# Row products of U on three places of their own, three picks moved to the later part of the pass, a buffer of its own for the last block

## The reference

```python
q = (xb @ w_q).reshape(T, PEER_HEADS, 2, PEER_QDIM // 2)
s = jnp.einsum('thpc,hpkc->thpk', q, sub_keys)          # scores against 2 x 128 keys per head
top_s, top_i = lax.top_k(s, PEER_TOPK)                  # 16 best keys of each half
cand = top_s[:, :, 0, :, None] + top_s[:, :, 1, None, :]
best_s, best_c = lax.top_k(cand.reshape(T, PEER_HEADS, PEER_TOPK * PEER_TOPK), PEER_TOPK)
ids = i1 * N_KEYS + i2                                  # 8 heads x 16 experts for each token
g = jax.nn.softmax(best_s, axis=-1)
act = jax.nn.gelu(jnp.einsum('td,thkd->thk', xb, u_tab[ids]), approximate=False)
out = jnp.einsum('thk,thkd->td', g * act, v_tab[ids])
```

## Time and profile before

| | us |
|---|---|
| median of 3 runs | 2987.31 (2981.48 to 2988.35) |
| the profiled execution, its own time | 2983.09 |
| its span, first to last instruction | 2981.3 |
| TensorE busy | 2801.1 (94%) |
| VectorE busy | 2345.2 (79%) |
| GpSimd busy | 1576.7 (53%) |
| ScalarE busy | 969.3 (33%) |
| mean granted TensorE clock | 0.964 of full speed |

### The profile page before, as it was taken

One profiled execution on the slowest core, in us unless ns is written; L12 is line 12 of the kernel. 1 busy time (PEld: TensorE's weight loads), 2 busy tenths in 40 slices (PEclk: granted clock), 3 DMA queues, 4 the chain that ended last, 5 costly groups with the idle time before them and its releaser, 6 DMA issues.

```text
span 2981.3 us, 33747 instructions
## 1 busy us (share of the span) xinstructions
PE 2801.1 (94%) x12016; PEld 2151.1 (72%) x12016; DVE 2345.2 (79%) x3821; ACT 969.3 (33%) x1331; POOL 1576.7 (53%) x1235
## 2 busy tenths in 40 slices
PE   7999689999688899999979999999999999999998
PEld 3546544788567688888767777777777777777776
DVE  2787943587999977777568888888888888888886
ACT  2014232311144466666222323223223223232233
POOL 1999400011011265666157777777777777777640
PEclk9999589999899999999989999999999999999999
DMA  3111010212335599999998888889888888898883
GB/s 121 39 46 54 3 43 0 78 43 78 130 121 170 162 332 366 366 362 362 351 339 304 301 305 317 296 301 317 301 303 310 300 306 308 298 320 288 317 290 142
DMA packets 253976, 685.16 MB, mean 230 GB/s; under 512 B 31984, under 2 KB 97648, under 8 KB 248432
## 3 DMA queue, kind: packets, MB, share of 16 engines
q0 software_dynamic: 104448, 335.81, 32.4%
q1 hardware_dynamic: 83568, 313.65, 28.6%
q10 hardware_dynamic: 65792, 33.56, 3.9%
HBM read 611.60 MB, written 71.30 MB: 229 GB/s over the span
## 4 chain that ended last, share of the span: by engine, by line
PE 66%; DVE 24%; DVEq 3%; issue 2%; DMA 2%; ACT 2%; another core or an unknown queue 1%; SPq 0%; ACTq 0%
PE ps L1604 21%; PE ps L1596 14%; PE ps L1569 11%; PE ps L1527 6%; DVE ps L1214 6%; DVE hnT L895 4%; PE ps L1455 3%; PE ps L1555 3%; PE ps L1364 2%; DVE ul L1187 2%; DVE wl L1284 1%; PE ps L1324 1%; DMA u_raw<-in_uT 1%; DVE lx L1061 1%; PE ps L1419 1%
## 5 line engine op out<-in xcount | busy, mean ns | idle before, releaser
L523 POOL DMA_INDIRECT vring<-in_v_tab,idsA x512 | 547.3, 1069 | 323.9 <-DVE ps L1214 193.9
L1214 DVE SCALAR_TENSOR_TENSOR ps<-vring,hsel,ps 128x1024 f32<-128x1024 f32 x508 | 652.0, 1283 | 15.3 <-DVE ps L1214 0.5
L512 POOL DMA_INDIRECT hsel<-hidden,idsE x384 | 436.8, 1138 | 159.8 <-issue 109.0
L1604 PE MATMUL ps<-vh,wh 128*128 128x512 f32 x1024 | 403.8, 394 | 28.4 <-DVE wl L1284 28.4
L1596 PE MATMUL ps<-xh,uh 128*128 128x512 f32 x1024 | 408.3, 399 | 12.0 <-DVE ul L1187 11.4
L1604 PE MATMUL ps<-vh,wl 128*128 128x512 f32 x1024 | 405.7, 396 | 0.0
L1596 PE MATMUL ps<-xh,ul 128*128 128x512 f32 x1024 | 405.1, 396 | 0.0
L1604 PE MATMUL ps<-vl,wh 128*128 128x512 f32 x1024 | 403.6, 394 | 0.0
L1596 PE MATMUL ps<-xl,uh 128*128 128x512 f32 x1024 | 402.7, 393 | 0.0
L1569 PE MATMUL ps<-hx,xh 128*128 128x512 f32 x768 | 314.5, 410 | 52.9 <-DVE lx L1061 51.6
L498 POOL TENSOR_TENSOR hot<-marks,selG 128x1024 f32<-128x1024 bf16 x64 | 140.1, 2190 | 364.6 <-PE ps L1555 227.0
(11 more groups left out here) (187 smaller groups left out, 4960.7 us busy)
## 6 DMA issues: line engine op xcount, KB each, us to landing
xraw<-in_uX SPq DMA_DIRECT2D x128, 512.0 KB, 6.5
u_raw<-in_uT SPq DMA_DIRECT2D x128, 512.0 KB, 7.3
v_raw<-in_v_tab SPq DMA_DIRECT2D x128, 512.0 KB, 5.4
gates<-gbuf ACTq DMA_DIRECT2D x16, 2048.0 KB, 23.7
gt<-gates SPq DMA_DIRECT2D x32, 1024.0 KB, 7.6
hidden<-hst SPq DMA_DIRECT2D x96, 256.0 KB, 8.1
wqbuf<-in_w_q SPq DMA_DIRECT2D x16, 512.0 KB, 3.4
vring<-in_v_tab,idsA POOLq DMA_INDIRECT x512, 5.8
```

The costliest lines, as they stand in the source:

```text
L512: nc.gpsimd.indirect_dma_start(out=hsel[:, n, k:k + 1], out_offset=None, in_=hidden_items, in_offset=bass.IndirectOffsetOnAxis(ap=idsE[:, ...
L523: nc.gpsimd.indirect_dma_start(out=vring[r % VS][:, :], out_offset=None, in_=v_rows if r >= P else u_rows, in_offset=bass.IndirectOffsetOn ...
L1214: nc.vector.scalar_tensor_tensor(out=bank2(6), in0=vring[slot][:, :], scalar=w, in1=bank2(6), op0=ALU.mult, op1=ALU.add).then_inc(cb_done, 1)
L1604: last = mm(ps[:, 2 + k % 4, :], w[:, c, tt * P:(tt + 1) * P], v[:, c, dh * 512:(dh + 1) * 512], start=c == 0 and w is wh and v is vh, sto ...
```

## The change

1. **Picks.** `picks_done` now spreads five picks (tiles 0, 4, 5, 6, 7; 70 steps) over quarters 0 to 35, and the other three (tiles 1, 2, 3; 42 steps) over quarters 36 to 121.
2. **Hot blocks** stand five quarters later: 21 + 1.5 n, quarters 21 to 115.
3. **Dots** run from quarter 41 to 126, 1.49 a quarter. Their rows have three places (`uring`, the places 2, 4 and 6 of `vring`) instead of eight, and semaphores of their own (`u_got`, `dot_read`). The fetch of a dot stands two quarters before it in GpSimd's list, and from the fourth on it waits until the dot three before it is done. The fetches of V rows count from zero again and begin when all dots are done.
4. **Last block.** The results of block 31 of the pass go to a buffer of their own, `hlast`, and the store has a semaphore of its own. So the first piece of the gates (`gt`, which lies where `hst` was) is loaded before these stores and no longer behind them.
5. `exps` stands one quarter earlier in ScalarE's list relative to its pick; some small tiles (`cand2`, `idf`, `best`, ...) have other addresses. The way back of `xh` and `xl` stays behind the stores of block 29 in SP's list.

```diff
-PICK_QUARTERS = 44
-X_BLOCK = PICK_QUARTERS // QB - 1
-X_QUARTER = PICK_QUARTERS + 4
+FIRST_PICKS = 1 + HT
+FIRST_QUARTERS = 36
+LAST_PICK = QUARTERS - 6
+X_BLOCK = FIRST_QUARTERS // QB - 1
+X_QUARTER = FIRST_QUARTERS + 4
 DOT_FROM = X_QUARTER + 1
+DOT_SLOTS = (2, 4, 6)
+US = len(DOT_SLOTS)
...
-def picks_done(qb):
-    return min(NT * STEPS_PICK, NT * STEPS_PICK * (qb + 1) // PICK_QUARTERS)
+def picks_done(Q):
+    first = FIRST_PICKS * STEPS_PICK
+    if Q < FIRST_QUARTERS:
+        return first * (Q + 1) // FIRST_QUARTERS
+    return min(NT * STEPS_PICK, first + (NT * STEPS_PICK - first) * (Q + 1 - FIRST_QUARTERS) // (LAST_PICK - FIRST_QUARTERS))
...
 def hot_quarter(n):
-    return 16 + n * 3 // 2
+    return 21 + n * 3 // 2
...
+        uring = [vring[k] for k in DOT_SLOTS]
+        hlast = at(0, "hlast", [P, PT, WIDTH])
...
             def store_hidden(B):
                 for n in range(PT):
                     e = B * PT + n
                     sp.wait_ge(h1_free, e + 1)
-                    sp.dma_start(hidden[n * P:(n + 1) * P, B * WIDTH:(B + 1) * WIDTH],
-                                 hst[:, e % HSLOTS, :]).then_inc(hst_out[e % HSLOTS], 16)
+                    dst = hidden[n * P:(n + 1) * P, B * WIDTH:(B + 1) * WIDTH]
+                    if B == NB - 1:
+                        sp.dma_start(dst, hlast[:, n, :]).then_inc(hlast_out, 16)
+                    else:
+                        sp.dma_start(dst, hst[:, e % HSLOTS, :]).then_inc(hst_out[e % HSLOTS], 16)
...
                 if B == NB - 1:
                     for c in range(2):
                         sp.wait_ge(lx_ready, QUARTERS - QB + c + 1)
                         sp.dma_start(u_raw[:, c, :], uT[c]).then_inc(u_in[c], 16)
+                    for slot in range(HSLOTS):
+                        sp.wait_ge(hst_out[slot], 16 * stores(slot))
+                    load_gates(0)
                 store_hidden(B)
-                if B == hot_quarter(HT * BLOCKS - 1) // QB + 2:
+                if B == hot_quarter(HT * BLOCKS - 1) // QB + 1:
...
-            def gather_row(r):
-                if r >= VS:
-                    pool.wait_ge(cb_done, r - VS + 1)
-                elif r == VS - 2:
+            def gather_dot(k):
+                if k == 0:
+                    pool.wait_ge(ids_ready, 1)
+                    pool.wait_ge(sel_ready, FIRST_PICKS)
+                elif k >= US:
+                    pool.wait_ge(dot_read, k - US + 1)
+                else:
                     pool.wait_ge(xt_ready, 1)
...
                 nc.gpsimd.indirect_dma_start(
+                    out=uring[k % US][:, :], out_offset=None, in_=u_rows,
+                    in_offset=bass.IndirectOffsetOnAxis(ap=idsA[:, 0, k:k + 1], axis=0)).then_inc(u_got[k % US], 16)
...
-                while Q > X_QUARTER - 3 and rows < min(ITEMS, items_done(Q + 3)):
-                    gather_row(rows)
-                    rows += 1
+                for k in range(P):
+                    if quarter_of_dot(k) - 2 == Q:
+                        gather_dot(k)
...
             def dot(k):
-                dve.wait_ge(v_got[k % VS], 16 * (k // VS + 1))
-                row = vring[k % VS][:, :]
+                dve.wait_ge(u_got[k % US], 16 * (k // US + 1))
+                row = uring[k % US][:, :]
                 nc.vector.scalar_tensor_tensor(out=row, in0=row, scalar=1.0, in1=bank2(6), op0=ALU.mult, op1=ALU.mult,
-                                               accum_out=hsel[:, 0, k:k + 1]).then_inc(cb_done, 1)
+                                               accum_out=hsel[:, 0, k:k + 1]).then_inc(dot_read, 1)
```

More of the change, by code:

```diff
@@ L110, with stores @@
 AX = mybir.AxisListType
-def picks_done(qb):
-    return min(NT * STEPS_PICK, NT * STEPS_PICK * (qb + 1) // PICK_QUARTERS)
+def picks_done(Q):
[3 more added lines that the diff above has]
+    return min(NT * STEPS_PICK, first + (NT * STEPS_PICK - first) * (Q + 1 - FIRST_QUARTERS) // (LAST_PICK - FIRST_QUARTERS))
 def quarter_of_step(k):
-    return next(qb for qb in range(PICK_QUARTERS) if picks_done(qb) > k)
+    return next(Q for Q in range(QUARTERS) if picks_done(Q) > k)
+def stores(slot):
+    return len(range(slot, (NB - 1) * PT, HSLOTS))
 def share(total, parts, n):
@@ L126, in hot_quarter, with dots_done, quarter_of_dot @@
 def hot_quarter(n):
-    return 16 + n * 3 // 2
-def items_done(Q):
-    return min(ITEMS, share(ITEMS, QUARTERS - 1 - DOT_FROM, max(0, Q + 1 - DOT_FROM)))
-def quarter_of_item(r):
-    return next(Q for Q in range(QUARTERS) if items_done(Q) > r)
+    return 21 + n * 3 // 2
+def dots_done(Q):
+    return min(P, share(P, QUARTERS - 1 - DOT_FROM, max(0, Q + 1 - DOT_FROM)))
+def quarter_of_dot(k):
+    return next(Q for Q in range(QUARTERS) if dots_done(Q) > k)
 def row_of_step(step):
@@ L375, in load_x, with load_gates @@
                 sp.dma_start(xraw[:, r, :, :], uX[b, :, r * KQ:(r + 1) * KQ, :]).then_inc(xraw_in[r], 16)
+            def load_gates(g):
+                sp.dma_start(gt[:, :, :, :], gates[g]).then_inc(g_in, 16)
             def store_hidden(B):
@@ L440, in load_group @@
                     sp.dma_start(v_raw[:, c % VR, :], v_tab[g * GC + c]).then_inc(v_in[c], 16)
-                    if c == (0 if first else 1):
-                        if first:
-                            for slot in range(HSLOTS):
-                                sp.wait_ge(hst_out[slot], 16 * (NB * PT // HSLOTS))
-                        else:
-                            sp.wait_ge(w_ready, g * GC)
+                    if c == 1 and not first:
+                        sp.wait_ge(w_ready, g * GC)
                         load_gates(g)
@@ L1254, in _ @@
                     marked += 1
-                for r in range(items_done(Q - 1) if Q else 0, items_done(Q)):
-                    if r < P:
-                        dot(r)
-                    else:
-                        combine(r - P)
+                for k in range(dots_done(Q - 1) if Q else 0, dots_done(Q)):
+                    dot(k)
             for c in range(2):
```

74 lines of the change are left out of this document (39 added, 35 removed).

## The result

| | before | after |
|---|---|---|
| median, us | 2984.39 (2980.73 to 2988.35, 4 runs) | 2945.44 (2939.84 to 2955.07, 4 runs) |
| ratio, 95% interval | | 0.9874 [0.9848, 0.9901] |
| the profiled execution, its own time | 2983.09 | 2955.07 |
| its span | 2981.3 | 2953.3 |

The change gains 39 us, 1.3%, and the interval keeps clear of no change; 2950 us was forecast. The profiled execution is the slowest of its four runs and gains 28 us. So I use a second profiled execution of the same program as well, taken beside the experiments ("after again", own time 2945.49). Of these two the second stands for the median.

A forecast was written before the change was run, and what follows sets the result against it. VectorE's picks were taken to bound quarters 4 to 43 and TensorE quarters 43 to 126. The terms, 42 − 8 + 0 + 3 = 37 us, put the median at 2950 us, range 2933 to 2975.

The forecast's parts named there:

- term 2: Three places for U rows, quarters 41 to 126: the loop of three dots loses 8 us, bounds 0 to 35.
- Term 1: Picks moved out of quarters 4 to 43: quarter 43 starts at 994, 42 us gained, bounds 36 to 47.
- are hidden: Later quarters: VectorE's idle 1.3 us a quarter covers the 42 moved steps, 0.9 us a quarter (75 us).
- mean P = 10.9: Mean time of one turn of three dots, in us; turns were to cost nothing up to 10.7.
- Term 3: Load of quarter 127 behind the last gates piece: piece takes 32 us, wait stays 5 us, change 0, bounds +6 and −21.
- my formula: Before quarter 127: TensorE waits if the last gates piece takes over 26.9 us to land.
- Term 4: Hand-over to the next pass: `gt` no longer waits behind the last stores, 3 us gained, bounds 0 and 5.
- The ring, mildly: Rival: fetches land after 9.8 to 10 us, the three places lose 26 to 35 us, 2968 to 2977; chance 0.12.
- Badly: Rival: a turn of three dots takes over 11.8 us, slower than before, 3007 us at 12.2; chance 0.08.
- Late gates: Rival: the last gates piece takes 53 us again, TensorE waits 26 us before quarter 127, 2971 us; chance 0.09.
- VectorE bounds the later part: Rival: scalings and picks collide or uneven steps keep TensorE waiting, 20 us of the picks' gain lost, 2970; chance 0.07.

The follow-up runs named there:

- repeats, 8 places: Changed kernel without picks of tiles 1 to 3, with 64 repeated `lx` operations in quarters 41 to 120 and eight places: 3052.7 us, ratio 0.9869.
- dots by time: Changed kernel with 116 dots in quarters 41 to 115 and 12 in quarters 116 to 126: 2944.19 us, ratio 0.9879.
- gates behind stores: Changed kernel with the first load of `gt` back behind the last three stores and the wait for them: 3060.14 us, ratio 0.9899.
- repeats, 3 places: Changed kernel without picks of tiles 1 to 3, with 64 repeated `lx` operations in quarters 41 to 120, three places: 3061.77 us, ratio 0.9898.

## Why the prediction was right, and where it was wrong

The total was right, but partly by luck: term 2 was mis-sized (−21 us for −8), and terms 1, 3 and 4 together came out better than forecast by about as much. With −21 in term 2 and the other terms as forecast the gain would have been 24 us. In the second execution (span 37.6 us shorter) the terms measure as follows; the profiled first one in brackets.

**Term 1, the picks that move: 42 forecast, +49.0 (+46.3) measured.** Quarter 43 starts at 987.3 (990.0) instead of 994, with 15 blocks done as said: 54.3 us earlier less three blocks of 1.78. In the first execution the first wait for `lx` was 16.35 us, 17 forecast, and all of TensorE's waits up to 1041.6 us together 19.9, under 30:

```profile
787.43 0.80 PE L1592 MATMUL ps<-hx,xh 128*128 128x512 f32 x1 [16.35 <-DVE lx L1087]
```

Only two short ones follow it. Quarter 36 started at 948.9 (951.7) us, 956 forecast, so my 1.78 us a step and 3 us for uneven steps together were a little too dark; the second execution is 2 us above the upper bound of 47.

**The moved steps "are hidden": this and term 2 is where the working failed.** The idle 79.6 us of the earlier trace rows were counted twice: once as cover for 42 steps, once as VectorE's freedom to start up to three quarters ahead while the ring turns. The ring without the late picks is free up to quarter 116 (0.2 us of excess); with them, or with plain operations of the same length, the excess is some 10 us above before. Work without the narrow ring was not free either in the one run that has it (repeats, 8 places: 6.8), so how the 10 us split between the two is not shown. A late row holds VectorE up, and what stands behind it, now with a pick step among it, no longer catches up before TensorE asks.

**Term 2, the three places: −8 forecast, −21.0 (−28.5) measured,** within its bounds (0 to −35). I put into it all that TensorE lost between quarter 43 and 127, though the late picks have a part in it. It is the excess up to quarter 116, 9.8 (11.4) above before, and that of quarters 116 to 127 without a wait at 127, 11.2 (17.0) above before. Fetches landed after 8.2 us, in the 7 to 9 forecast, and GpSimd did wait for dots. What I had wrong is the part of the ring in the tail. There TensorE needs only 8.3 us for three dots; I named that number and yet laid the whole of it into one mean P = 10.9 over 43 turns. The median hid that fetches in the chain of the tail landed after 6.6 to 15.9 us (first execution); the 15.87 one was issued 1.1 us behind the first of the two 2 MB loads:

```profile
1427.50 0.74 SPq L439 DMA_DIRECT2D xh<-x_rows  x1
1428.29 0.81 SPq L440 DMA_DIRECT2D xl<-x_rows  x1
```

My own test for this was "quarter 126 ends more than 15 us behind quarter 43's start + 437": it ended 22.6 (30) behind. By that test I was wrong.

**Term 3, the way to quarter 127: 0 forecast, +5.7 (+4.9) measured,** near its upper bound of +6. The last piece of the gates was issued at 1396.23 and landed after 27.9 us, 32 forecast and 53.3 before:

```profile
gates<-gbuf ACTq DMA_DIRECT2D x1, 2048.0 KB, 27.9
```

The limit for no wait was 26.9 us, so by my formula 1 us was to be left, and 0.87 was. That match is luck. The load of quarter 127 was issued at 1429.5 and took 20.2 us, so it had landed by 1449.7; the 0.87 us are the end of the wait for a late row, whose dot at 1455.33 stands in VectorE's list before the `lx` at 1456.69. TensorE came 11 to 17 us later to quarter 127 than its own work needs, so the load had that much more time. Where TensorE does not lose that time, the wait before quarter 127 is there: 8.54 and 6.45 us without late picks (3 and 8 places), 7.99 in "dots by time", 8.75 in "repeats, 8 places", against 5.73 before. So terms 2 and 3 don't add up independently: the ring's loss in the tail hides a wait for this load of 6 to 9 us. What the change cost the tail is better read as one number: excess 11.4 (18.1) against 5.9.

The Trainium skill (DMA: Bandwidth & Descriptors, "Queues, rings and completion order") has each DMA engine take turns between queues with work; by that rule three places were to bring this term to +6. The piece did land sooner, but runs made for other questions show that it needs no three places. With the new tables, eight places and no late picks the last piece landed after 31.7 us, though the 15 row fetches from 1369 to 1393 us took 8.8 to 17.0. And with three places and the old tables it was issued at 1418.3, and its queue moved nothing more from 1450 on, so under 32 us. Either change alone goes with some 32 us instead of 53.3; why, these runs don't separate further.

**Term 4, the hand-over: +3 forecast, about +4.3 measured:** 2.1 us from quarter 127 to the first matmul with U, 2.2 us from there to the first with V. Only the second half is what I had forecast, and "gates behind stores" speaks for the load's place as its cause. The first half I had not foreseen, and it belongs to the wait before quarter 127: behind its 5.7 us wait the granted clock was 0.65 of full from 1480 to 1487 us, a mixture of its two levels (1.2 and 2.4 GHz), and 1.00 from 1446.9 to 1451.9 us in the second execution, which had no such wait. The wait of the first V matmul fell from 13.70 to 12.41 us:

```profile
1492.96 0.80 PE L1627 MATMUL ps<-vh,wh 128*128 128x512 f32 x1 [12.41 <-DVE wl L1307]
```

**The sum** of the second execution: 49.0 − 21.0 + 5.7 + 4.3 = 38.0 against 37.6 of its span; of the first: 46.3 − 28.5 + 4.9 + 4.6 = 27.3 against 28.0, the rest being the pass over V. The terms are differences of starts in one pair of traces, so they must add up; that they do says nothing on the causes.

**The rivals.** "The ring, mildly" had the price nearly right for the first execution (26 to 35 us forecast, 28 measured), but not the mechanism: it laid the loss into the whole stretch, where it needs the late picks beside it, and more than half of it arises where hot blocks are missing. "Badly" did not come: even with the denser old table the loss was 12 us. "Late gates" is refuted by the 27.9 us. "VectorE bounds the later part" named the cover that failed, but laid its price, 20 us, on term 1, which lost nothing.

**What the tail hangs on.** Between quarter 116 and the pass over V, 50 us of TensorE's work take 56 to 69 us in every run of the table, whichever wait was removed. Fetches late: take four dots away, and the load of quarter 127 is late; put the load first as well, and the first loads of U are late; and so in the kernel before, with a ratio of 1.0003. That moving one wait uncovers another is shown. Two common causes are open. One is the filled DMA engines (share 0.95). The other is the order of SP's list: the load of quarter 127, or the first loads of U, stand behind the wait for the last piece of the gates and a burst of 4 MB. No run took bytes out of the tail, and none let the first loads of U pass the burst.

## What to carry to other kernels

Idle time of an engine is one stock: before two changes are both called hidden by it, subtract the first and ask what is left for the second. When terms of a forecast share a stretch, look whether the loss of one hides a wait of another; a total that comes out right does not show it. A ring that waits for its reader must be sized at its tightest place (here the quarters without hot blocks, with a 4 MB burst beside them), not by the mean pace and the median landing time. And where several transfers share full DMA engines ahead of one hand-over, putting another first may only move the wait (here it did in two runs); look at the time across the hand-over, not at the wait that went.

## What the runs showed of the hardware

- **A VectorE operation with two inputs in SBUF runs longer beside GpSimd's scaling, and not beside its row fetches.** The means look as if fetches did it. The repeated `lx` with three places and with eight (groups on VectorE, 990 to 1390 us; busy us, mean ns):

```profile
L1088 DVE TENSOR_TENSOR lx<-xraw,hx 128x1024 fp32r<-128x1024 f32 x57 | 75.2, 1319 | 0.5
```

```profile
L1088 DVE TENSOR_TENSOR lx<-xraw,hx 128x1024 fp32r<-128x1024 f32 x58 | 97.4, 1680 | 0.5
```

  But the marks of the same two runs go the other way, 1773 with three places and 1438 with eight. And a `picks` operation beside fetches in the changed kernel (first line, 1090 to 1408.3 us) has the same mean as in the kernel before, where the four in the second line (990 to 1390 us) ran before the first row fetch was issued:

```profile
L1148 DVE TENSOR_TENSOR picks<-ranks,iota 128x2048 bf16<-128x2048 bf16 x4 | 8.1, 2075 | 0.2
```

```profile
L1122 DVE TENSOR_TENSOR picks<-ranks,iota 128x2048 bf16<-128x2048 bf16 x4 | 8.1, 2074 | 0.2
```

  The single operations tell it apart. In each of the 14 traces, from 990 to 1390 us, every `lx`, mark and large `picks` operation (128x2048) that meets no scaling in time takes 1.17 to 1.29 us, also where it meets a fetch being issued (at most 1.29). Beside a scaling (1.9 us at the least) it takes up to 3.6. One such pair, in "repeats, 3 places", VectorE and then GpSimd:

```profile
1040.40 2.92 DVE L1213 TENSOR_TENSOR marks<-selI,iota 128x2048 bf16<-128x2048 bf16 x1
```

```profile
1040.02 2.22 POOL L514 TENSOR_TENSOR hot<-marks,selG 128x1024 f32<-128x1024 bf16 x1
```

  The dot, with one input of its two in `ps`, stays at 1212 to 1217 ns in all of them. The Trainium skill's rule (SBUF — State Buffer, "SBUF: two separate sides") says this: two inputs in SBUF and a GpSimd operation that reads SBUF exclude each other, and these traces agree. What a change of tables does to a mean is then which operations happen to meet a scaling. From 990 to 1390 us such operations took some 54 us more than 1.22 each in "repeats, 8 places", 33 in "repeats, 3 places", 15 to 16 in the changed kernel and 23 before; so part of the 6.8 us excess with eight places may be these meetings. I had put 0.1 us on each moved operation.
- **The same kernel took 2981 us at one time and 3090 at two others.** In the variants profiled beside the slower ones, the pass over U keeps its times and the extra time lies in the pass over V, where DMA moved 279 GB/s in one of them (repeats, 3 places, 1560 to 2900 us) against 304 before. The same chip is on record for 2981 and for one of the 3090, so the chip does not explain it; the cause is open.
